# Dilated attention: where each head pair's values product stands among TensorE's work

## What is computed

```python
q, k = rope(q, pos), rope(k, pos)
pool_out = multi_scale_pool(u_pool, w_pool[l], pool_scale[l])
attn_out = dilated_attention(q, k, v).reshape(B, S, ATTN_WIDTH)
mix = jnp.concatenate([pool_out, attn_out], axis=-1) @ w_out[l]
...
# dilated_branch, three branches (128, 1), (512, 4), (2048, 16)
s = jnp.where(valid[None, None, :, None], s, -jnp.inf)
m = jnp.max(s, axis=-1, keepdims=True)
e = jnp.exp(s - m)
den = jnp.sum(e, axis=-1, keepdims=True)
o = jnp.einsum('brnqhd,brnkhd->brnhqk', ...)   # scores, then probabilities times values
```

## Time and profile before

| | |
|---|---|
| median of 3 runs | 1959.91 us (1959.9 to 1960.38) |
| the profiled execution's own time | 1960.69 us |
| its span in the profile | 1958.9 us |
| PE busy | 1952.4 us, 100% of the span |
| PE weight loads | 1601.0 us, 82% |
| DVE, ACT, POOL busy | 909.8 us (46%), 815.5 us (42%), 768.7 us (39%) |
| stage 1 of the attention, scores to next scores | 59.59 to 84.55 us |
| stage 3 | 108.66 to 133.65 us |
| stage 5, from its scores | from 157.76 us |

### The profile page before, as it was taken

How to read it: one execution, slowest core, us unless ns; L and a number is a source line. 1 busy time by engine, 2 the same in 40 slices (tenths; PEclk the granted TensorE clock), 3 DMA queues, 4 the chain that set the end, 5 groups by cost and what they waited for, 6 DMA issues and landing times.

```text
span 1958.9 us, 26026 instructions
## 1 busy us (share of the span) xinstructions
PE 1952.4 (100%) x9055; PEld 1601.0 (82%) x9055; DVE 909.8 (46%) x1184; ACT 815.5 (42%) x1098; POOL 768.7 (39%) x307
## 2 busy tenths in 40 slices
PE   9999999999999999999999999999999999999999
PEld 6777888888888888888888888888777788888887
DVE  5775654343146456454243434224788764343200
ACT  6664533232244433434332323225888752323211
POOL 4223444444424334343444444443222244444443
PEclk9999999999999999999999999999999999999999
DMA  5212122222323222222232223232111122222322
GB/s 173 73 64 90 65 97 96 96 96 103 103 73 115 80 86 91 70 96 75 93 100 96 96 96 113 89 99 85 55 64 53 55 97 96 96 96 96 110 98 93
DMA packets 49012, 177.39 MB, mean 91 GB/s; under 512 B 5568, under 2 KB 6464, under 8 KB 48960
## 3 DMA queue, kind: packets, MB, share of 16 engines
q1 hardware_dynamic: 46656, 172.95, 26.2%
q10 hardware_dynamic: 2304, 3.74, 0.6%
HBM read 174.57 MB, written 2.10 MB: 90 GB/s over the span
## 4 chain that ended last, share of the span: by engine, by line
PE 98%; DVE 1%; ACT 0%; DMA 0%; issue 0%; SPq 0%; DVEq 0%; ACTq 0%
PE B L363 26%; PE B L364 26%; PE B L372 26%; PE B L1277 2%; PE B L1085 1%; PE B L1089 1%; PE B L1086 1%; PE B L384 1%; PE B L389 1%; PE B L385 1%; PE B L1266 1%; PE B L1322 1%; PE B L913 1%; PE B L944 1%; PE B L929 1%; PE B L1131 1%
## 5 line engine op out<-in xcount | busy, mean ns | idle before, releaser
L608 POOL TENSOR_TENSOR WL<-RAW,WH 128x1024 fp32r<-128x1024 f32 (+1 forms) x296 | 757.7, 2562 | 1162.5 <-PE B L372 753.1
L363 PE MATMUL B<-HH,WH 128*128 128x512 f32 x1608 | 628.2, 391 | 0.3 <-DVE QT L2195 0.3
L364 PE MATMUL B<-HL,WH 128*128 128x512 f32 x1608 | 626.1, 389 | 0.0
L344 ACT CAST WH<-RAW 128x1024 fp32r<-128x1024 f32 (+1 forms) x300 | 329.1, 1098 | 521.4 <-PE B L364 444.6
L372 PE MATMUL B<-HH,WL 128*128 128x512 f32 x1608 | 398.3, 390 | 0.0
L363 PEld LDWEIGHTS B<-HH,WH 128*128 128x128 f32 x1608 | 301.8, 188 | 64.8 <-issue 1.7
L372 PEld LDWEIGHTS B<-HH,WL 128*128 128x128 f32 x1608 | 301.4, 188 | 63.2 <-POOL WL L608 0.5
L364 PEld LDWEIGHTS B<-HL,WH 128*128 128x128 f32 x1608 | 301.9, 188 | 62.3
L1963 DVE TENSOR_TENSOR U<-B,RB 128x512 f32<-128x512 f32 x66 | 45.6, 691 | 294.3 <-PE B L372 294.3
L363 PE MATMUL B<-MH,WH 128*128 128x512 f32 x440 | 171.2, 389 | 0.0
L364 PE MATMUL B<-ML,WH 128*128 128x512 f32 x440 | 171.2, 389 | 0.0
(11 more groups left out here) (392 smaller groups left out, 2376.9 us busy)
## 6 DMA issues: line engine op xcount, KB each, us to landing
RAW<-in_w_small SPq DMA_DIRECT2D x254, 512.0 KB, 3.2
RAW<-in_w_large SPq DMA_DIRECT2D x48, 704.0 KB, 4.0
out_t<-X SPq DMA_DIRECT2D x7, 256.0 KB, 4.4
X<-in_x_t ACTq DMA_DIRECT2D x4, 256.0 KB, 6.8
X<-in_x_t SPq DMA_DIRECT2D x4, 256.0 KB, 7.1
DECAY<-in_decay ACTq DMA_DIRECT2D x4, 256.0 KB, 2.6
RAW<-in_w_small ACTq DMA_DIRECT2D x2, 256.0 KB, 7.1
RAW<-in_w_small SPq DMA_DIRECT2D x2, 256.0 KB, 7.9
```

The source lines that it names most:

```text
L344: act.copy(wh, raw).then_inc(s_hi, 1)
L363: pe.matmul(bank, wh[:, c, :], xh[:, k0 + c, :], start=(start and c == 0), stop=False)
L364: mm = pe.matmul(bank, wh[:, c, :], xl[:, k0 + c, :], start=False, stop=False)
L608: pool.tensor_tensor(wl, raw, wh.bitcast(F32), ALU.subtract).then_inc(s_lo, 1)
```

## The change

In the stages where pair a - 1 is not one of `POOL_ENDS`, that is a = 1, 3 and 5, `values(a - 1)` is called between `scores()` and `turn_v()`. In stages 2 and 4 it stays where it was. The turns of probabilities and all other engines' lists are the same.

```diff
+                values_late = a is not None and a - 1 in POOL_ENDS
                 if a is not None:
                     scores()
+                    if not first_a and not values_late:
+                        values(a - 1, 1 - ap)
                     turn_v()
                 if j is not None:
                     if not first:
...
                     low_part(pe, u, B[0][:], DC, HH)
                 if a is not None:
-                    if not first_a:
+                    if values_late:
                         values(a - 1, 1 - ap)
                     if j is None:
                         some_out(0, range(0, 5))
```

## The result

The change takes 1964.68 us (median of 12 runs, 1964.33 to 1968.91), the kernel before 1960.3 us beside it (12 runs, 1959.88 to 1960.65): 4.4 us more, ratio 1.0024 with a 95% interval of 1.0015 to 1.0033 (the medians by themselves stand at 1.0022; one run of 1968.91 us lies far above the others). Forecast were 1964.4 us, and 4.5 us of loss. The profiled run took 1964.73 us, its span is 1963.0 us.

The account below looks back on a forecast made before the run. PE, busy for the whole span, was taken to bound the kernel. Losses of 1.43 us in stages 1 and 3 each and 1.6 in stage 5 summed to 4.5, on 1959.9 giving 1964.4 us; range 1961.0 to 1965.7.

Parts of the forecast that it names:

- PE's list is the time: Whole kernel: PE is always busy, so a reorder gains only switching costs and loses any PE wait it makes.
- What is late: Stage 1, ACT: the chain from the split waiting for Q's high part up to M1H moves by 2.31 us.
- POOL's split first, the sum behind it: Stage 1: POOL's split starts at 76.03 to 76.13, DVE's pool sum comes at 76.27 and is held until 78.97.
- the row of L2172: Stage 1, DVE: a product of two SBUF tensors beside POOL took 1.45 us, ending 0.55 behind POOL's end.
- the order of the two hardly matters: Stage 1: were DVE ahead of POOL, its second sum would be held instead, at the same price or 0.2 more.
- Where PE meets it: Stage 1, PE: waits at the second turn and pool product make the next scores 1.43 us late, again in stage 3.
- Stage 5: Exponentials follow the late V copy, 1.84 to 1.94 us late; PE waits at both turns, +1.6 us (1.6 to 1.7).
- The seams: PE in stages 1, 3 and 5: the new order saves about 0.2 us of switching in each, if PE never waits.
- The first, sums not held: Rival: POOL does not hold the sums; stages 1 and 3 gain 0.2 each, stage 5 loses 1.6; 1961.1 us; 14%.
- The second, seams only: Rival: the change brings only its seams, -0.6 us, 1959.3 us, needing 1.8 us of slack in stage 5; 6%.
- The third, L2178 losing to POOL as well: Rival: the pool differences in stages 1 and 3 also wait for POOL, 2.6 us more each, 1969.6 us; 9%.
- the chance of 0.61: Chance of slower by over 0.2%: all of the POOL-held differences rival and about 8 in 10 of the forecast.

Follow-up runs that it names:

- the run with stage 5 alone: Values product moved behind the scores in stage 5 only, against the kernel before: 1961.65 us, ratio 1.0008 (0.9999 to 1.0017), 1.46 us more.
- the last mended kernel: The change, with DVE's pool sums behind the masks and, in stage 5 only, ACT's V copy behind both heads' exponentials; against the kernel before: 1959.4 us, ratio 0.9997.
- the other mended kernel: The change, with DVE's pool sums behind the masks and ACT's V copy behind head 0's exponentials; against the kernel before: 1959.71 us, ratio 0.9998.
- stages 1 and 3 alone: Values product moved behind the scores in stages 1 and 3 only, against the kernel before: 1963.24 us against 1960.19, ratio 1.0016.

## Why the prediction was right

The forecast was right in its sign, its size and its steps.

- **PE's list is the time.** The losses of the stages, 26.41 - 24.96 = 1.45, 26.42 - 24.99 = 1.43 and 15.52 - 13.84 = 1.68, come to 4.56 us; less the 0.36 of an earlier start this is 4.20, and the span is 4.1 longer. Nothing was given back later.
- **What is late.** ACT's split starts 6.75 us behind the scores before (59.59) and 9.06 us behind them now (59.23): 2.31 later, as forecast. M1H follows without a pause.
- **POOL's split first, the sum behind it.** Forecast were 0.14 to 0.24 us between them, measured 0.32 (75.60, 75.92): the cast starts 0.48 us behind the start of M1H, where I took 0.49 to 0.59, and POOL followed the cast's end by 0.10 where I took 0.15. The hold ended 0.55 behind POOL, as taken from the row of L2172; the sum took 2.62 us, forecast was 78.97 - 76.27 = 2.7. This was the one price that no row of the sum itself showed, a choice between two values; reading one input from PSUM took it away, and with it the loss of stages 1 and 3. That the order of the two hardly matters (DVE first, the second sum held instead) was claimed as well, and no run tests it. The Trainium skill's page "SBUF — State Buffer" ("Who interferes with whom") says just this of two SBUF inputs against one, and the runs agree, 2.62 us against 0.68.
- **Where PE meets it.** Waits of 0.9 and 0.5 us were forecast in front of the second turn and the pool product; 0.86 and 0.37 stand in the rows. 1.43 us was forecast for the stage, 1.45 and 1.43 were measured. The 0.1 us for weights that aren't loaded ahead after a wait is in the rows too: the pool product takes 1.12 us for 1.02, and its first weights are loaded from 84.58 on, with the matmul itself; before they were loaded from 83.37, ahead of the product at 83.60.
- **Stage 5.** 1.6 forecast, 1.68 in the profile, 1.46 by the medians of the run with stage 5 alone. The exponentials were to be 1.84 to 1.94 late and are 1.83. The first turn waits 0.95 us, where I had said about 1.1. Putting the exponentials ahead of the copy, or the transposes of V ahead of the values, takes the loss away but for 0.33 and 0.00 us.
- **The seams.** 0.2 us in each stage were to be saved. With PE's waits removed, stages 1 and 3 are 24.71 and 24.75 for 24.96 and 24.99: 0.25 and 0.24; stage 5 is 13.68 for 13.84, 0.16.
- **The rivals.** The first, sums not held, was made real by the PSUM input: 1.1 us above the kernel before, where 1.2 had been worked out. The second, seams only, is what the last mended kernel shows: 0.65 us less by its stages, 0.84 by the medians, for 0.6; the other mended kernel still has a wait in stage 5 and doesn't count for it. The third, L2178 losing to POOL as well, did not come: the differences start at 83.84, POOL at 84.29 (0.45 behind, 0.4 forecast), and they take 0.69 us.

A median at 1964.4 was called just beyond 0.2%. The measured one is there too, but its interval, 1.0015 to 1.0033, shows only that there is a loss, not that it is over 0.2%; the chance of 0.61 for that is neither borne out nor refuted. Some of the closeness is luck: the forecast of the time stands on 1959.9 us for the kernel before, which ran at 1960.3 beside the change, and the parts hit within 0.1 us where each was allowed 0.1 to 0.3. The mechanism doesn't rest on that: a sum held for 2.62 to 2.63 us, with PE's two waits behind it and stages of 26.4 to 26.6 us, repeats in four kernels (the change, stages 1 and 3 alone, exponentials ahead of the copy, transposes of V first).

## What to carry to other kernels

When one engine is busy all the time, a reorder on it is worth no more than its seams, and its price is found elsewhere: follow each list that waits for the rows that have become later, until that list comes back to the busy engine. A step that was hidden may have to pass another engine's instruction on its new way; look at what stands beside its new place, not only at its old duration. Filling work like the pool's sums belongs where its engine waits anyway and no neighbour holds what it reads.

## What the runs showed of the hardware

- A DVE sum of two SBUF tensors started 0.32 us behind a POOL instruction and took 2.62 us, until 0.55 us after POOL's end; with one input from PSUM it took 0.68 us at the same distance.
- The place of the values product (128 rows by 64 columns of the array) matters by 0.2 us: directly behind the scores (64 rows by 128) stages 1 and 3 take 26.41 and 26.42 us, behind the 128 by 128 transposes 26.63 and 26.62, with the same waits.
- An instruction of DVE with a single SBUF tensor as input can be held by POOL too, so not having a second one, as in the sum above, does not help everywhere. The four L2239 that normalise a head took 1.28 us with POOL idle and 1.78 beside its split, in the changed kernel. The first of the four took 0.79 us instead of 0.29, until 0.08 behind POOL's end:

```profile
67.61 1.28 DVE L2239 TENSOR_SCALAR PR<-PR,RD 128x128 f32<-128x128 f32 x4
...
71.78 1.78 DVE L2239 TENSOR_SCALAR PR<-PR,RD 128x128 f32<-128x128 f32 x4
```

```profile
70.09 2.40 POOL L608 TENSOR_TENSOR WL<-RAW,WH 128x1024 fp32r<-128x1024 f32 x1 [8.29 <-PE B L372]
```
